# Two Strassen MLPs on one core: block sums of the weights by adding loads, another order of the products, moved embedding parts

## The chip, the cores and the metric

One core of one Trainium2 chip runs the whole kernel. The metric is the device time of one execution in microseconds (us), and fewer is better. Five engines work in parallel, each through its own in-order list of instructions, and wait for each other by semaphores: PE (TensorE, matrix products), DVE (VectorE), ACT (ScalarE), POOL (GpSimd) and SP (SyncE, which only issues transfers here). POOL can issue transfers too.

## The reference

Two transformer blocks follow each other on x of 512 tokens by 1024 features, all in float32. Each has a mixer, which the change leaves alone, and then this:

```python
x = x + merged @ w_out                                   # "wo"
h = rmsnorm(x, g)
x = x + square(relu(h @ w_ff1)) @ w_ff2                  # w_ff1 [1024, 4096], w_ff2 [4096, 1024]
gate = sigmoid(rmsnorm(x, g3) @ w_gate)                  # "pg"
x = x + (p @ w_ple) * gate                               # p [512, 256], the embedding part
```

The second block does the same with weights of its own (`w_mlp1_2`, `w_mlp2_2`, `w_pg_2`, `w_pp_2`), and a final rmsnorm gives the output.

## The kernel before

**Precision.** A float32 product is made of three products of parts with fewer bits: every operand is split into a high part (a copy on ACT: `wh`, `SH`, `XH`, `YH`) and a low part (a subtraction on DVE: `wl`, `SL`, `XL`, `YL`), and PE adds high*high, high*low and low*high in a PSUM bank. Weights arrive as raw chunks of 1 MB (`raw`, two buffers, issued by SP) and are split in units of 128 x 1024 elements. `wh` and `wl` have three buffers (`NW = 3`), so a unit is converted when the unit three ahead of it has been used by PE (`ac_hi`, `dv_lo`, event `wfree`). A unit feeds 24 matmuls, or 12 where it is half of a product.

**First layer.** `dense_mlp` runs the eight blocks of `wo`, then the hidden features in four groups (g = 0 to 3) of eight blocks `f1` each. ACT makes relu and square into `hid`.

**Second layer.** For each group the product of `hid` (512 tokens by 1024) with 1024 rows of `w_ff2` is done by Strassen's method: seven products of quarters (M1 to M7) instead of eight. The weights' quarters lie in four tiles `RB` (11, 12, 21, 22, of 1 MB each), loaded by SP in `sp_second`. Four of the seven products need a sum of two weight quarters; DVE makes it in place (`dv_weight_sums`, two halves each). Four operand sums on DVE (`dv_operands`: into `E` and in place in `hid`) make the other side. `PRODUCTS` gives for each product the pair of banks, whether it starts them afresh (otherwise it adds on), and the quarter of the output `xt` (tokens th, features nh, sign) into which DVE adds the banks (`dv_mlp`, event `f2e`).

The products of group g lie between the `f1` blocks of group g + 1, one after each. The last group has no such blocks: its seven products stand one after another, with two embedding parts (`ple`: one unit, 24 matmuls each) after the third and the sixth.

**Around it.** The rows of p are loaded by POOL (`pl_ple`, tile `prows`), transposed by PE (`pe_ple`) and split into `PPH` and `PPL`. When a quarter of `xt` is complete, PE transposes it (`pe_turn`, order `TURN`), DVE adds it to `XT` (first MLP), and the gate product `pg` follows (`fm_lead`, three blocks which begin with features 4 to 7). In the second MLP the turned quarters are split straight from the banks, and the gate product is `pg2`. The scale `rst1` for the gate comes from squares (ACT), their sum in `ACC` (DVE) and a product with ones; `dv_gate` needs it before it frees a bank.

**Order.** Each engine has lanes of steps (`vector_lanes` and the like). A planner (`arrange`) runs through them with costs and due times of its own and writes out one fixed order for each engine; conversions are due by the place at which PE needs them. A step that waits holds up everything behind it on its engine.

```python
us = [self.unit(self.RB[q][:, 2 * h:2 * h + 2, :], 2, 512, ("rb", blk, g, q) if kind == "rb" else ("ts", blk, g, k, h)) for h in range(2)]
...
if u["i"] >= NW:
    ac.wait_ge(self.at("wfree", u["i"] - NW))
```

## Time and profile before

| | |
|---|---|
| runs before (3) | 1928.93, 1932.8, 1934.3 us, median 1932.8 |
| profiled execution | 1934.82 us |
| its span, first to last instruction | 1933.0 us |
| PE busy | 1883.5 us, 97% |
| PE weight load, beside it | 1551.5 us |
| DVE busy | 1151.1 us, 60% |
| ACT busy | 855.3 us, 44% |
| POOL busy | 98.8 us, 5% |
| mean granted clock | 0.989 |

The profile is of one execution. "Busy" is the time with an instruction of the engine under way. "PEclk" is the granted share of TensorE's full clock in a stage. In a row of a stage the number in brackets behind a busy time is how many instructions started in it. A wait names the engine and the tile that came last. The first MLP lies at about 464 to 866 us, the second at about 1476 to 1878 us.

### The profile page before, as it was taken

To read this page: it belongs to the slowest core of one execution; us is meant where nothing else is said; L and a number is where in the kernel's file an instruction comes from. 1 tells how busy PE (TensorE), PEld (TensorE's weight loads), DVE (VectorE), ACT (ScalarE), POOL (GpSimd) and SP (SyncE) were. 2 spreads that over 40 slices of the span, in tenths; PEclk is the share of its full clock that TensorE was granted. 3 is DMA by queue.
4 is the path that set the end of the run, shared out by engine and by line. 5 is a ranking of instruction groups with operands and counts; after the bars stand their busy time and mean duration, and the time that the engine had idled before them with its cause. 6 is when DMAs were issued, how large, how long until landed. Compare 5 with 4: busy or idle time off the path is not lost.

```text
span 1933.0 us, 23466 instructions
## 1 busy us (share of the span) xinstructions
PE 1883.5 (97%) x9426; PEld 1551.5 (80%) x9426; DVE 1151.1 (60%) x1777; ACT 855.3 (44%) x1318; POOL 98.8 (5%) x153
## 2 busy tenths in 40 slices
PE   7999999998999999899999999999999999999897
PEld 5887778877788888778888888898887888888786
DVE  5769665446456857788734335424345456857775
ACT  6435554323344444456634324333233444445363
POOL 2110111002000000000100000000000000000000
PEclk9999999999999999899999999999999999999999
DMA  6233211129423232212431222232255223232211
GB/s 226 66 91 119 85 55 40 45 78 328 127 66 110 87 131 87 87 44 79 142 117 47 88 69 85 92 105 82 93 196 185 87 66 122 81 124 89 97 44 65
DMA packets 158175, 194.65 MB, mean 101 GB/s; under 512 B 14826, under 2 KB 118932, under 8 KB 158067
## 3 DMA queue, kind: packets, MB, share of 16 engines
q1 hardware_dynamic: 151954, 181.91, 29.2%
q0 software_dynamic: 4528, 8.94, 1.4%
q10 hardware_dynamic: 1584, 2.30, 0.3%
q8 instruction: 75, 1.23, 0.3%
q14 instruction: 34, 0.27, 0.0%
HBM read 179.41 MB, written 15.54 MB: 101 GB/s over the span
## 4 chain that ended last, share of the span: by engine, by line
PE 87%; DVE 7%; ACT 2%; DMA 2%; issue 2%; POOL 0%; POOLq 0%; DVEq 0%; SPq 0%; ACTq 0%
PE bank L131 84%; PE bank L134 3%; DVE wl L155 1%; DMA prows<-in_p_dram 1%; ACT L141 1%; ACT wh L141 1%; DVE ACC L155 1%; DVE T L155 1%; DVE RB L155 0%; DMA scr_x<-XT 0%; DVE XL L163 0%; DVE XT L155 0%; ACT GP L141 0%; DVE ML L155 0%; DVE xt L163 0%
## 5 line engine op out<-in xcount | busy, mean ns | idle before, releaser
L131 PE MATMUL bank<-XH,wh 128*128 128x512 f32 (+1 forms) x1272 | 504.1, 396 | 5.3 <-DVE XL L163 2.2
L131 PE MATMUL bank<-XL,wh 128*128 128x512 f32 (+1 forms) x1272 | 497.0, 391 | 1.0 <-DVE XL L163 1.0
L141 ACT ACTIVATE wh<-raw 128x1024 fp32r<-128x1024 f32 (+1 forms) x239 | 252.8, 1058 | 534.2 <-PE bank L131 526.2
L155 DVE TENSOR_TENSOR wl<-raw,wh 128x1024 fp32r<-128x1024 f32 x238 | 292.8, 1231 | 269.6 <-ACT wh L141 269.1
L131 PE MATMUL bank<-XH,wl 128*128 128x512 f32 x1264 | 318.7, 394 | 0.0
L131 PEld LDWEIGHTS bank<-XH,wh 128*128 128x128 f32 (+1 forms) x1272 | 238.8, 188 | 60.5 <-issue 2.6
L131 PEld LDWEIGHTS bank<-XL,wh 128*128 128x128 f32 (+1 forms) x1272 | 238.9, 188 | 51.0 <-DVE XL L163 2.4
L131 PEld LDWEIGHTS bank<-XH,wl 128*128 128x128 f32 x1264 | 236.3, 189 | 49.6 <-issue 0.6
L141 ACT ACTIVATE wh<-RB 128x1024 fp32r<-128x1024 f32 x112 | 119.1, 1063 | 158.6 <-PE bank L131 158.6
L155 DVE TENSOR_TENSOR wl<-RB,wh 128x1024 fp32r<-128x1024 f32 x112 | 137.0, 1223 | 76.5 <-ACT wh L141 76.4
L131 PE MATMUL bank<-wh,SL 128*128 128x512 f32 x448 | 140.2, 395 | 12.6 <-DVE SL L155 12.6
L131 PE MATMUL bank<-wh,SH 128*128 128x512 f32 x448 | 139.6, 393 | 0.0
L131 PE MATMUL bank<-wl,SH 128*128 128x512 f32 x448 | 139.3, 392 | 0.0
L131 PEld LDWEIGHTS bank<-wh,SL 128*128 128x128 f32 x448 | 85.2, 191 | 31.1 <-DVE SL L155 13.5
L131 PEld LDWEIGHTS bank<-wl,SH 128*128 128x128 f32 x448 | 85.2, 190 | 18.0
L131 PEld LDWEIGHTS bank<-wh,SH 128*128 128x128 f32 x448 | 84.6, 190 | 17.6
L163 DVE SCALAR_TENSOR_TENSOR xt<-bank,scales,xt 128x512 f32<-128x512 f32 x104 | 77.7, 747 | 4.1 <-DVE xt L163 0.9
L155 DVE TENSOR_TENSOR RB<-RB,RB 128x1024 f32<-128x1024 f32 x64 | 78.2, 1221 | 1.4
L155 DVE TENSOR_TENSOR T<-bank,RST 128x512 f32<-128x512 f32 x58 | 40.0, 689 | 60.6 <-PE bank L131 60.3
L131 PE MATMUL bank<-wh,XH 128*128 128x512 f32 x192 | 60.4, 396 | 0.0
L131 PE MATMUL bank<-wh,XL 128*128 128x512 f32 x192 | 59.7, 392 | 0.0
L131 PE MATMUL bank<-wl,XH 128*128 128x512 f32 x192 | 59.7, 392 | 0.0
(446 smaller groups left out, 2583.7 us busy)
## 6 DMA issues: line engine op xcount, KB each, us to landing
raw<-in_w_in_dram SPq DMA_DIRECT2D x58, 1024.0 KB, 5.2
RB<-in_w_ff_dram SPq DMA_DIRECT2D x16, 1024.0 KB, 5.0
raw<-in_w_ff_dram SPq DMA_DIRECT2D x16, 1024.0 KB, 5.3
RB<-in_w_mlp_dram SPq DMA_DIRECT2D x16, 1024.0 KB, 5.1
raw<-in_w_mlp_dram SPq DMA_DIRECT2D x16, 1024.0 KB, 5.3
raw<-in_w_out_dram SPq DMA_DIRECT2D x8, 1024.0 KB, 5.2
scr_x<-XT POOLq DMA_DIRECT2D x16, 256.0 KB, 4.6
XT<-scr_x SPq DMA_DIRECT2D x8, 512.0 KB, 10.9
```

Of the source, the lines that this page charges most:

```text
L131: return self.put(ns, lambda e: e.matmul(out, lhsT, rhs, start=start, stop=stop, skip_group_check=True))
L134: return self.put(109, lambda e: e.transpose(out, in_, ident))
L141: return self.put(ns, lambda e: e.activation(out, in_, func, bias=bias, scale=scale), func)
L155: return self.put(self.ns(out), lambda e: e.tensor_tensor(out, a, b, op))
L163: return self.put(self.ns(out), lambda e: e.scalar_tensor_tensor(out, a, s, b, op0, op1))
```

## The change

- `dv_weight_sums` on DVE goes. In its place POOL issues loads that add to what lies in the tile (`dma_add`, `accum_op`): for each of the four sums the second quarter is read from DRAM again and added to the first in `RB`, in two halves of 512 KB (`pl_weight_sums`, lane `tsum`, in the order sum 1, 3, 2, 4). Sum 3 waits for the load of quarter 12, the others until the low part of the plain weights in the tile has been made.
- The quarters 11 and 12 change tiles from group to group, and SP loads in the order 22, 11, 21, 12.
- The order of the products was M1, M2, M5, M6, M3, M7, M4 and is M1, M5, M6, M3, M7, M2, M4. M2 has banks 4 and 5 and not 6 and 7. The operand sum for M3 is made after the second operand (M6) has been split.
- The embedding parts stand ahead of the first and the second product of the last group. Their raw chunk is planned ahead of that group's products.
- The transposes of `prows` wait for the last block of `wo` too.
- Quarters are turned in the order 12, 22, 11, 21. In the first MLP ACT's squares come in fours behind the copies.
- After the first MLP the ring of banks for `pg` has a fourth one, bank 3.

```diff
--- before.py
+++ after.py
@@ -195,6 +195,13 @@
 
     def idle(self):
         return [self.last] if self.e is not None and self.last else []
+
+    def dma_add(self, out, in_):
+
+        if self.e is None:
+            self.notes.append(("dma", self.dma_ns, 8 * int(np.prod(in_.shape))))
+            return Noted(self.notes)
+        return self.e.dma_start(out, in_, accum_op=ALU.add)
 
     def power(self, out, a, b):
         return self.put(500 + 250 * size(out), lambda e: e.tensor_tensor(out, a, b, ALU.pow))
@@ -533,13 +540,14 @@
         yield from self.fm_lead(s, "Y", [("pg", n) for n in range(3)])
         for n in range(3, 8):
             yield from self.fm(s, "Y", ("pg", n))
+        self.ring = (0, 1, 2)
         yield from self.fm_pair(s, "X2", ("ha",), ("gqk", 0, 0))
         for pr in range(2):
             for c in range(2):
                 for i in range(2):
                     if (pr, c, i) != (0, 0, 0):
                         yield from self.fm(s, "X2", ("gqk", c, 2 * pr + i))
-        yield from self.tm(s, "X2", ("gv", 0), [("xm", 0, 3, 7)])
+        yield from self.tm(s, "X2", ("gv", 0), self.last_use[3])
         yield from self.tm(s, "X2", ("gv", 1), [("free", "gv", 0, 3)])
         for g in range(3):
             for pr in range(2):
@@ -580,11 +588,12 @@
                 yield from self.fm(s, x, ("f1", blk, g + 1, n))
                 if n < 7:
                     yield from self.product(s, blk, g, n)
+
         for i in range(7):
+            if i < 2:
+                yield from self.ple(s, blk, i)
             yield from self.product(s, blk, 3, i)
-            if i in (2, 5):
-                yield from self.ple(s, blk, i == 5)
-        self.ring, self.last_use[2] = (0, 1, 2), self.pair_after[2]
+        self.ring, self.last_use[2], self.last_use[3] = (0, 1, 2) if blk else (0, 1, 2, 3), self.pair_after[2], self.pair_after[3]
 
     def ple(self, s, blk, hf):
         if blk == 0:
@@ -1773,11 +1782,11 @@
     def plan_ff(self, blk, w1, wp):
         for j in range(4):
             self.plan("f1", w1, 0, 8, 256 * j, 256, "n", 2)
-        made = ((11, "rb", 11), (21, "rb", 21), (11, "ts", 1), (11, "ts", 2), (22, "rb", 22), (12, "ts", 3), (21, "ts", 4))
+        made = ((11, "rb", 11), (11, "ts", 1), (11, "ts", 2), (22, "rb", 22), (12, "ts", 3), (21, "rb", 21), (11, "ts", 4))
 
         def product(g, i):
             q, kind, k = made[i]
-            us = [self.unit(self.RB[q][:, 2 * h:2 * h + 2, :], 2, 512, ("rb", blk, g, q) if kind == "rb" else ("ts", blk, g, k, h)) for h in range(2)]
+            us = [self.unit(self.RB[g][q][:, 2 * h:2 * h + 2, :], 2, 512, ("rb", blk, g, q) if kind == "rb" else ("ts", blk, g, k, h)) for h in range(2)]
             self.f2_units.setdefault((blk, g), []).append(us)
         for g in range(3):
             for n in range(8):
@@ -1786,12 +1795,11 @@
                 self.piece(ci, "n", 2, n % 2)
                 if n < 7:
                     product(g, n)
+        ci = self.chunk(wp, 0, 2, 0, 1024)
         for i in range(7):
+            if i < 2:
+                self.piece(ci, "n", 2, i)
             product(3, i)
-            if i == 2:
-                ci = self.chunk(wp, 0, 2, 0, 1024)
-            if i in (2, 5):
-                self.piece(ci, "n", 2, i == 5)
 
     def sp_spill1(self, s):
         sp = self.sp
@@ -1876,7 +1884,10 @@
         self.xt = m("xt", 16, [128, 4, 1024])
         self.SH = [m("SH", 24 + 4 * i, [128, 4, 256], F32R) for i in range(2)]
         self.SL = [m("SL", 26 + 4 * i, [128, 4, 256], F32R) for i in range(2)]
-        self.RB = {q: m("RB", 32 + 4 * i, [128, 4, 512]) for i, q in enumerate((11, 12, 21, 22))}
+
+        RB = [m("RB", 32 + 4 * i, [128, 4, 512]) for i in range(4)]
+        self.RB = [{11: RB[g % 2], 12: RB[1 - g % 2], 21: RB[2], 22: RB[3]} for g in range(4)]
+        self.RB_SLOT = [{11: g % 2, 12: 1 - g % 2, 21: 2, 22: 3} for g in range(4)]
         self.E = self.page("E", P_SCAN, [128, 4, 256])
         YA, YB = [m("YA", 4 * i, [128, 4, 512], F32R) for i in range(2)], [m("YB", 8 + 4 * i, [128, 4, 512], F32R) for i in range(2)]
         self.YH, self.YL = [[YB[i][:, k, :] for k in range(4)] + [YA[i][:, k, :] for k in range(4)] for i in range(2)]
@@ -1907,8 +1918,8 @@
 
 
 
-    PRODUCTS = (("M1", (2, 3), True, 0, 0, 1), ("M2", (6, 7), True, 0, 0, 1), ("M5", (4, 5), True, 1, 1, 1), ("M6", (2, 3), False, 0, 1, -1),
-                ("M3", (4, 5), False, 0, 1, 1), ("M7", (2, 3), False, 1, 1, -1), ("M4", (2, 3), False, 1, 0, 1))
+    PRODUCTS = (("M1", (2, 3), True, 0, 0, 1), ("M5", (4, 5), True, 1, 1, 1), ("M6", (2, 3), False, 0, 1, -1), ("M3", (4, 5), False, 0, 1, 1),
+                ("M7", (2, 3), False, 1, 1, -1), ("M2", (4, 5), True, 0, 0, 1), ("M4", (2, 3), False, 1, 0, 1))
 
     def quarter(self, g, th, kh):
         return self.hid[g % 2][:, 4 * kh:4 * kh + 4, 256 * th:256 * th + 256]
@@ -1916,13 +1927,13 @@
     def operand(self, g, i):
 
         q = self.quarter
-        return (q(g, 0, 0), q(g, 0, 1), self.E[:, :, :], q(g, 0, 0), q(g, 0, 1), q(g, 1, 0), q(g, 1, 1))[i]
+        return (q(g, 0, 0), self.E[:, :, :], q(g, 0, 0), q(g, 0, 0), q(g, 1, 0), q(g, 0, 1), q(g, 1, 1))[i]
 
     def operand_made(self, blk, g, i):
-        tiles = {0: range(4), 1: range(4, 8), 6: range(4, 8)}.get(i)
+        tiles = {0: range(4), 5: range(4, 8), 6: range(4, 8)}.get(i)
         if tiles:
             return [self.at("hid", blk, g, n) for n in tiles]
-        return [self.at("ss", blk, g, {2: 1, 3: 2, 4: 4, 5: 3}[i])]
+        return [self.at("ss", blk, g, {1: 1, 2: 2, 3: 4, 4: 3}[i])]
 
     def ac_operands(self, s):
         ac = self.ac
...
@@ -1955,48 +1966,49 @@
                 dv.wait_ge(s.now())
                 dv.tensor_tensor(q(g, 1, 0), q(g, 0, 0), q(g, 1, 0), ALU.subtract).then_inc(*s.up(("ss", blk, g, 3)))
                 yield
-                self.splitting = x0 + 3
+                self.splitting = x0 + 2
                 dv.wait_ge(s.now(), at("sh", blk, g, 0))
                 dv.tensor_tensor(q(g, 0, 0), E, q(g, 0, 0), ALU.subtract).then_inc(*s.up(("ss", blk, g, 2)))
-                yield
-                low(1)
-                yield
-                self.splitting = x0 + 4
-                dv.wait_ge(s.now(), at("sh", blk, g, 1))
-                dv.tensor_tensor(q(g, 0, 1), q(g, 0, 1), q(g, 0, 0), ALU.add).then_inc(*s.up(("ss", blk, g, 4)))
-                for i in range(2, 7):
+                for i in range(1, 7):
                     yield
                     low(i)
-
-    def dv_weight_sums(self, s):
-
-        dv, at, RB = self.dv, self.at, self.RB
+                    if i == 2:
+                        yield
+                        self.splitting = x0 + 3
+                        dv.wait_ge(s.now(), at("sh", blk, g, 2))
+                        dv.tensor_tensor(q(g, 0, 0), q(g, 0, 1), q(g, 0, 0), ALU.add).then_inc(*s.up(("ss", blk, g, 4)))
+
+    def second(self, blk, g, q, k0=0, nk=4):
+
+        r0, c0 = 1024 * g + 512 * (q // 10 - 1) + 128 * k0, 512 * (q % 10 - 1)
+        return self.a[("w_ff2", "w_mlp2_2")[blk]][0][r0:r0 + 128 * nk, c0:c0 + 512].rearrange("(k p) n -> p k n", p=128)
+
+    def pl_weight_sums(self, s):
+
+        pl, at = self.pl, self.at
         for blk in range(2):
             for g in range(4):
-                part = lambda q, h: RB[q][:, 2 * h:2 * h + 2, :]
                 u = self.f2_units[blk, g]
-                for k, q, a, b, i, lows, loads in ((1, 11, 11, 12, 2, 0, (11, 12)), (3, 12, 12, 22, 5, None, (22,)), (2, 11, 11, 22, 3, 2, ()), (4, 21, 11, 21, 6, 1, (21,))):
+                for k, q, b in ((1, 11, 12), (3, 12, 22), (2, 11, 22), (4, 11, 21)):
                     for h in range(2):
                         yield
-                        self.splitting = u[i][h]
-                        dv.wait_ge(s.now(), *[at("rb", blk, g, x) for x in loads], *([at("lo", u[lows][h])] if lows is not None else []))
-                        dv.tensor_tensor(part(q, h), part(a, h), part(b, h), ALU.add).then_inc(*s.up(("ts", blk, g, k, h)))
+                        pl.wait_ge(at("rb", blk, g, q), *([] if k == 3 else [at("lo", u[{1: 0, 2: 1, 4: 2}[k]][h])]))
+                        pl.dma_add(self.RB[g][q][:, 2 * h:2 * h + 2, :], self.second(blk, g, b, 2 * h, 2)).then_inc(
+                            *self.sig(f"ts{self.RB_SLOT[g][q]}{h}").up16(("ts", blk, g, k, h)))
 
     def sp_second(self, s):
 
         sp, at = self.sp, self.at
-        for blk, name in enumerate(("w_ff2", "w_mlp2_2")):
-            w = self.a[name][0]
+        for blk in range(2):
             for g in range(4):
-                for q in (11, 22, 12, 21):
+                for q in (22, 11, 21, 12):
                     yield
                     if g:
-                        u = self.f2_units[blk, g - 1]
-                        sp.wait_ge(at("lo", u[{11: 3, 22: 4, 12: 5, 21: 6}[q]][1]), *{11: [at("ts", blk, g - 1, 4, 1)], 22: [at("ts", blk, g - 1, 2, 1)], 12: [], 21: []}[q])
+
+                        sp.wait_ge(at("lo", self.f2_units[blk, g - 1][{22: 3, 11: 4, 21: 5, 12: 6}[q]][1]))
                     else:
                         sp.wait_ge(at("l", ("MG", "MG2")[blk], 7), at("acc", ("pa", "ot")[blk], 7))
-                    r0, c0 = 1024 * g + 512 * (q // 10 - 1), 512 * (q % 10 - 1)
-                    sp.dma_start(self.RB[q][:, :, :], w[r0:r0 + 512, c0:c0 + 512].rearrange("(k p) n -> p k n", p=128)).then_inc(*self.sig(f"rb{q}").up16(("rb", blk, g, q)))
+                    sp.dma_start(self.RB[g][q][:, :, :], self.second(blk, g, q)).then_inc(*self.sig(f"rb{self.RB_SLOT[g][q]}").up16(("rb", blk, g, q)))
 
     def dv_mlp(self, s, blk):
         dv = self.dv
...
@@ -2040,23 +2052,23 @@
                 ac.activation(self.hid[g % 2][:, n, :], self.tile["f1", blk, g, n][:, :], ACT.Square).then_inc(*s.up(("hid", blk, g, n)))
 
 
-    TURN = ((11, 1), (12, 4), (22, 5), (21, 6))
+    TURN = ((12, 3), (22, 4), (11, 5), (21, 6))
     TURNED = (4, 5, 6, 7, 0, 1, 2, 3)
 
     def pe_turn(self, s, blk):
         pe = self.pe
-        free = {p: ("f2e", blk, 3, 1, p) for p in range(2)}
+        free = {p: self.FF_FREE[blk] for p in range(2)}
         for q, i in self.TURN:
             th, nh = q // 10 - 1, q % 10 - 1
             for p in range(2):
                 yield
-                pe.wait_ge(*[self.at("f2e", blk, 3, i, j) for j in range(2)], self.at(*free[p]))
+                pe.wait_ge(*[self.at("f2e", blk, 3, i, j) for j in range(2)], *[self.at(*e) for e in free[p]])
                 for f in range(2):
                     for j in range(2):
                         n = 4 * nh + 2 * p + f
                         t = pe.transpose(self.ps[6 + p][:, 256 * f + 128 * j:256 * f + 128 * j + 128], self.xt[:, 2 * th + j, 128 * n:128 * n + 128], self.ident[:, :])
                 t.then_inc(*s.up(("ft", blk, q, p)))
-                free[p] = ("fte", blk, q, p)
+                free[p] = [("fte", blk, q, p)]
 
     def dv_turn(self, s):
         dv = self.dv
...
@@ -2099,6 +2111,12 @@
             yield
             ac.wait_ge(self.at("xm", 0, 3, n))
             ac.copy(self.YH[n], self.XT[:, n, :], self.vec(gain, n)).then_inc(*s.up(("h", "Y", n)))
+            if n in (7, 3):
+                yield from self.ac_squares(s, n - 3)
+
+    def ac_squares(self, s, n0):
+        ac = self.ac
+        for n in range(n0, n0 + 4):
             yield
             ac.wait_ge(self.at("imb", 0), *(self.freed("ysq", n) if n != 4 else []))
             sq = self.tile["ysq", n] if n != 4 else self.ACC
@@ -2110,10 +2128,10 @@
             yield
             dv.wait_ge(self.at("h", "Y", n))
             dv.scalar_tensor_tensor(self.YL[n], self.XT[:, n, :], self.vec(gain, n), self.YH[n].bitcast(F32), ALU.mult, ALU.subtract).then_inc(*s.up(("l", "Y", n)))
-            if n != 4:
-                yield
-                dv.wait_ge(self.at("ysqd", n), s.now())
-                dv.tensor_tensor(self.ACC[:, :], self.ACC[:, :], self.tile["ysq", n][:, :], ALU.add).then_inc(*s.up(("ysa", n)))
+            for m in {7: (5, 6, 7), 3: (0, 1, 2, 3)}.get(n, ()):
+                yield
+                dv.wait_ge(self.at("ysqd", m), s.now(), *([self.at("ysqd", 4)] if m == 5 else []))
+                dv.tensor_tensor(self.ACC[:, :], self.ACC[:, :], self.tile["ysq", m][:, :], ALU.add).then_inc(*s.up(("ysa", m)))
 
 
     def pl_ple(self, s, blk, p):
@@ -2140,7 +2158,7 @@
         pe = self.pe
         for k in range(2):
             yield
-            pe.wait_ge(self.at("prw", blk))
+            pe.wait_ge(self.at("prw", blk), self.at("acc", "wo", blk, 7))
             for j in range(4):
                 t = pe.transpose(self.ps[5 + k][:, 128 * j:128 * j + 128], self.prows[:, j, 128 * k:128 * k + 128], self.ident[:, :])
             t.then_inc(*s.up(("ppT", blk, k)))
...
@@ -3050,7 +3068,6 @@
         yield "onorm", 1000, lambda s: self.chain(self.dv_attn_norm(s), self.dv_gla_norm(s))
         yield "lo", None, self.dv_lo
         yield "operands", None, self.dv_operands
-        yield "sums2", None, self.dv_weight_sums
 
     def scalar_lanes(self):
         yield "norms", 1000, lambda s: self.chain(self.ac_norms(s), self.ac_turn_x(s))
@@ -3079,6 +3096,7 @@
         yield "gna", 0, lambda s: self.pl_group_norm(s, 0)
         yield "gnb", 0, lambda s: self.pl_group_norm(s, 1)
         yield "onorm", 0, lambda s: self.chain(self.pl_attn_norm(s), self.pl_gla_norm(s), self.pl_last(s))
+        yield "tsum", 0, self.pl_weight_sums
         yield "merge", 500, lambda s: self.chain(self.pl_merge(s), self.pl_blank2(s))
         yield "spill", 2000, lambda s: self.chain(self.pl_params(s), self.pl_keep(s), self.pl_ple(s, 0, a["p"][0, 0]), self.pl_rel_bias(s), self.pl_copy_bias(s), self.pl_spill2(s), self.pl_load_bias(s),
                                                   self.pl_dil(s), self.pl_ple(s, 1, a["p_2"][0, 0]), self.pl_lnf(s))
@@ -3166,7 +3184,7 @@
                     return l.slack
                 if l.slack is None:
                     need, lead = {("dv", "lo"): (self.need_lo, 2500), ("ac", "hi"): (self.need, 5000), ("ac", "operands"): (self.s_need, 5000),
-                                  ("dv", "operands"): (self.s_need, 3500), ("dv", "sums2"): (self.need, 9000)}[eng, l.name]
+                                  ("dv", "operands"): (self.s_need, 3500)}[eng, l.name]
                     return max(t, clock["pe"]) + 227 * (need[l.unit_of[l.i]] - dense) - lead
                 return t + l.slack
             lane = min(go, key=due)[1]
```

## Rows read from the trace of the kernel before

**Rows 1.** Page, busy time of each engine over the whole span.

```profile
PE 1883.5 (97%) x9426; PEld 1551.5 (80%) x9426; DVE 1151.1 (60%) x1777; ACT 855.3 (44%) x1318; POOL 98.8 (5%) x153
```

**Rows 2.** Waits of PE: for whom, total us, times, longest us.

```profile
PE bank L131 <- DVE SL L155: 12.6, 2, 6.3
PE bank L134 <- DMA prows<-in_p_dram: 8.2, 2, 5.3
...
PE bank L134 <- DVE xt L163: 1.9, 2, 1.7
```

**Rows 3.** Stages at two last groups: time, engines' busy us (starts), PEclk, DMA share, GB/s.

```profile
812.00:816.00 4.00, 0.00 (x0) 0.00 (x0) 3.98 (x4) 0.00 (x0) 0.00 (x0) 0.50 0.00 0
816.00:820.00 4.00, 3.97 (x9) 3.15 (x10) 2.36 (x2) 0.00 (x0) 0.00 (x0) 0.50 0.02 4
820.00:824.00 4.00, 4.00 (x15) 3.21 (x14) 2.21 (x3) 1.06 (x1) 0.00 (x0) 0.74 0.00 0
...
1828.00:1832.00 4.00, 2.98 (x7) 2.40 (x8) 3.32 (x3) 0.00 (x0) 0.35 (x1) 0.50 0.00 0
1832.00:1836.00 4.00, 4.00 (x18) 3.25 (x18) 1.73 (x2) 1.15 (x2) 0.20 (x1) 0.95 0.39 133
```

**Rows 4.** Timeline, DVE and PE around the first SL wait: start, us.

```profile
811.83 0.74 DVE L163 SCALAR_TENSOR_TENSOR xt<-bank,scales,xt 128x512 f32<-128x512 f32 x1
812.49 1.22 DVE L155 TENSOR_TENSOR RB<-RB,RB 128x1024 f32<-128x1024 f32 x1
813.62 1.22 DVE L155 TENSOR_TENSOR hid<-E,hid 128x1024 f32<-128x1024 f32 x1
814.76 1.22 DVE L155 TENSOR_TENSOR SL<-hid,SH 128x1024 fp32r<-128x1024 f32 x1
...
816.03 1.22 PE L131 MATMUL bank<-wh,SL 128*128 128x512 f32 x2 [6.32 <-DVE SL L155]
...
826.68 1.03 PE L134 MATMUL bank<-ident,xt 128*128 128x128 f32 x8
```

**Rows 5.** Stages around the transposes of prows, both MLPs (columns as above).

```profile
470.00:475.00 5.00, 2.87 (x11) 2.68 (x12) 0.93 (x2) 1.20 (x2) 0.00 (x0) 0.55 1.05 362
475.00:480.00 5.00, 5.00 (x15) 2.66 (x14) 2.98 (x5) 3.14 (x4) 0.00 (x0) 0.77 0.83 304
...
1480.00:1485.00 5.00, 2.08 (x10) 1.51 (x9) 0.00 (x0) 0.00 (x0) 0.00 (x0) 0.92 1.05 385
1485.00:1490.00 5.00, 5.00 (x21) 4.28 (x20) 2.57 (x4) 2.79 (x5) 0.00 (x0) 0.73 1.05 387
```

**Rows 6.** Page, groups of instructions on the RB tiles.

```profile
L141 ACT ACTIVATE wh<-RB 128x1024 fp32r<-128x1024 f32 x112 | 119.1, 1063 | 158.6 <-PE bank L131 158.6
L155 DVE TENSOR_TENSOR wl<-RB,wh 128x1024 fp32r<-128x1024 f32 x112 | 137.0, 1223 | 76.5 <-ACT wh L141 76.4
...
L155 DVE TENSOR_TENSOR RB<-RB,RB 128x1024 f32<-128x1024 f32 x64 | 78.2, 1221 | 1.4
```

**Rows 7.** Stages: one undisturbed group, and the first MLP's last group.

```profile
640.00:721.60 81.60, 81.60 (x361) 67.57 (x360) 57.94 (x55) 39.14 (x45) 0.00 (x0) 1.00 0.32 103
...
805.80:866.00 60.20, 53.13 (x232) 42.78 (x230) 50.49 (x54) 30.98 (x38) 0.00 (x0) 0.91 0.06 18
```

**Rows 8.** DMA issues: count, KB each, median us to landing.

```profile
RB<-in_w_ff_dram SPq DMA_DIRECT2D x16, 1024.0 KB, 5.0
...
raw<-in_w_proj_b_dram SPq DMA_DIRECT2D x4, 512.0 KB, 3.7
...
scr_b<-scr_row POOLq DMA_DIRECT2D x2, 512.0 KB, 14.2
...
scr_b<-scr_row POOLq DMA_DIRECT2D x1, 768.0 KB, 5.7
```

**Rows 9.** Instructions on scr_b: duration ns, first and last start, time to landing.

```profile
L119 POOL DMA_DIRECT2D scr_b<-scr_row x3: 1082/1109/1162, 484.4 to 486.7; - x3
...
DMA to landing us min/median/max: 4.6/5.8/16.7
```

More of the change, by code:

```diff
@@ L1949, in dv_operands @@
                 yield
-                self.splitting = x0 + 2
+                self.splitting = x0 + 1
                 dv.wait_ge(s.now(), at("sl", blk, g, 0), at("ppT", blk, 1), *[at("hid", blk, g, n) for n in range(8)])
@@ L2193, in pe_norms @@
         yield from self.pe_turn(s, 0)
-        yield from self.pe_mean_squares(s, "rst1", self.ACC, self.ps[4], ("ysa", 3), ("ysqd", 4), ("f2e", 0, 3, 4, 0))
+        yield from self.pe_mean_squares(s, "rst1", self.ACC, self.ps[4], ("ysa", 3), ("ysqd", 4), ("f2e", 0, 3, 5, 0))
         yield from self.pe_spread(s, "rst1", self.T[2], self.ps[4], ("ms1",))
         yield from self.pe_mean_squares(s, "m1", self.ACC, self.ps[4], ("sqp", 7), ("rst1",))
-        yield from self.pe_mean_squares(s, "m2", self.ACC2, self.ps[5], ("sqp2", 7), ("f2e", 0, 3, 4, 1))
+        yield from self.pe_mean_squares(s, "m2", self.ACC2, self.ps[5], ("sqp2", 7), ("f2e", 0, 3, 5, 1))
         yield from self.pe_spread(s, "rstB", self.T[2], self.ps[4], ("m1",))
```

14 lines of the change are left out of this document (7 added, 7 removed).

## The prediction

> **What bounds the kernel now.** I read the busy shares first. TensorE (PE) is busy 97% of the span [rows 1], so time can only come out of PE's own idle time or its slow clock, and a saving on another engine counts only where PE waits for it. So the next view is who PE waited for [rows 2]: 12.6 us in two waits for SL (the low half of an operand, from VectorE), 8.2 us in two waits for the load of prows (the embedding rows), 1.9 us in two waits for xt (VectorE's eviction of the last product). These are 22.7 of PE's 49.5 idle us (1933.0 less 1883.5), and all three lie in the code that is changed.
>
> A wait costs more than its idle time, because the granted clock falls. The stages around the first SL wait show it: no matmul from 812 to 816, clock 0.50 until past 820, 0.74 to 824 [rows 3]. In an undisturbed group PE starts 361 matmuls in 81.6 us [rows 7], 0.226 us each, so a block of 24 takes 5.4 us. From 816.0 to 824 there are 24 where 5.4 us would do: 2.5 us lost at half clock, the 1.2 GHz level. In the second MLP 25 start between 1829.0 and 1836: 1.3 us lost [rows 3]. In the same way 18 matmuls and 8 transposes (8 in about 0.9 us at full clock [rows 4]) fill 472.1 to 480, where 5.0 us would do: 2.9 us lost; in the second MLP 31 starts take 7.1 us where 6.1 would do: 1.0 us lost [rows 5]. The waits and their slow clock together: 12.6 + 3.8 + 8.2 + 3.9 = 28.5 us.
>
> **Why PE waits for SL.** The timeline in front of the wait shows VectorE in one unbroken queue: an eviction (811.8), a weight sum RB (812.5), an operand sum (813.6), and only then SL of the second product (814.8), for which PE sits idle 6.3 us [rows 4]. The same rows give the price of a piece in such a queue, start to start: 0.66 us for an eviction, 1.14 for a piece of 1024 elements. The last group has no f1 blocks between its products, so VectorE is needed at twice the rate.
>
> **The sums leave VectorE.** 64 sums of 1.22 us go, 78 us of VectorE [rows 6]. In groups 0 to 2 that is worth nothing: there VectorE is busy 58 of 81.6 us and PE 81.6 of 81.6 [rows 7]. In the last group two things remove the SL wait: the weight sum in the queue goes, and, more important, the first embedding block now lies ahead of product 0 and the second between products 0 and 1. hid is complete some 4 us before product 0 starts (f1 block 7 ends 5.4 us ahead, relu and square take 1.3), SL of product 1 then follows E, two sums and at most five other pieces, about 10 us, that is at +6 us, and product 1 starts at +10.9. Worth both waits and their clock: 12.6 + 3.8 = 16.4 us.
>
> What the denser end costs: from the start of product 1 PE has 6 products (32.6 us) and three turned quarters (16 transposes, 1.9 us each), 38 us. VectorE has in it 13 splits wl, 5 SL and one operand sum (1.14 each), 10 evictions and 4 YL (0.66 each), 6 additions to XT and 3 to ACC (0.6 each, an estimate from the eviction's size): 21.7 + 9.2 + 5.4 = 36.3 us. That is 95%; before, it was 50.5 of 60.2 us with the idle time of the wait in it [rows 7]. Bounds 0 and 4 us per MLP; I take 1.
>
> **The sums become adding loads.** Eight per group, 512 KB each, issued by GpSimd, whose queue is empty in both MLPs. The trace has no adding load. Its cost has two parts: a fixed latency, and an occupancy X by which the next one is later. A plain MB lands in 5.0 us, a plain half MB in 3.7 [rows 8]; I take 1.45 us per half MB and 2.1 fixed. If the add means that the target is read as well, two passes make 2.9 and three 4.4. The slowest row on this queue are the three copies scr_b, 1.75 MB from DRAM to DRAM, issued from 484.4 to 486.7 and landed within 16.7 us of issue: 19 us, less 2.1, is 4.8 us per half MB, with other loads beside them [rows 8, 9]. So X lies between 1.45 and 4.8; I take 3: source and target kind are those of the plain load, with one more pass. The issue itself is some 0.8 us of an idle engine.
>
> What waits for them: weight halves are converted three units ahead (wh has 3 buffers, and ScalarE's conversions of RB waited 158.6 us, all for PE [rows 6]). With product 0 at S: its two low halves are made at S-5.8 and S-3.0 (a unit is freed, then 1.06 + 1.22 + 0.1 us; S-8.5 for the first in the last group). The GpSimd lane is in order: sum 1 (two halves), sum 3 (two), sum 2. Sum 2's first half is needed 1.3 us before product 2: at S+20.5 in groups 0 to 2, at S+15.0 in the last. The backlog lands it at S-3.7+5X and S-0.9+4X: in time up to X = 4.8 and X = 4.0. At X = 3 it arrives 4 us early in the last group. Cost 0. Extra traffic: 4 MB per group of 81.6 us beside a DMA share of 0.32 [rows 7]; weight chunks are fetched about 24 us ahead of their use and land in 5, so nothing of PE's moves.
>
> "Collectives: The Full Stack" of the Trainium skill (The bandwidth ceiling) says that an add in the DMA path is slow not for the add but for its two source reads, about half the rate of a copy. By it X would be about 2.9 us, an estimate from that page; no trace here shows it.
>
> **The transposes of prows wait for the last wo product.** Before, they stood in PE's order where the load was still under way. Now PE goes on with wo, seven more blocks, some 38 us; the load, 5.3 us late before, has landed long by then. Gain 8.2 + 3.9 = 12.1 us. What is late next: wo's weights are fetched as far ahead as all chunks; the bias copies (scr_b) move with the transposes, to the start of f1, where a chunk beside them may take as long as they did, 16.7 us [rows 9], inside its 24. PPH and PPL have eight f1 blocks, 44 us, before a product asks for the banks. Cost 0.
>
> **Product order, turn, fourth bank.** Same matmuls and evictions. M7 and M4, on the same banks, are no longer neighbours. The quarters for chunks 4 to 7 are now finished at product 4 instead of 5, so the first gate half has its inputs 5.4 us earlier and can cover the last eviction, where PE waited 1.9 us: gain 0 to 3 with its share of the issue gaps, I take 1.5. ScalarE's squares are put after the copies, which makes rst1 2 to 3 us later; bank 3 lets PE do one more gate block (5.4 us) meanwhile. Cost 0, and without that bank some 2 us.
>
> **Sum.** 16.4 + 12.1 + 1.5 - 2 = 28 us. The profiled execution took 1934.8 (span 1933.0): 1906.8. It is 2.0 above the median of the runs, so the forecast is 1905. Its own range is 1899 to 1912.
>
> **Rivals.** (a) *The last group's wait comes back as a wait for sum 2.* X between 4.0 and 5: at 4.8 the half lands at S+18.3, 3.3 us late, with a slow clock 6.3 us, twice: 1905 + 13 = 1918. For it: the lane's fixed order and the densest place. Against it: X would have to be near that of DRAM-to-DRAM copies. Chance 0.16. (b) *VectorE still sets the end.* At 95% its splits come late: 4 us per MLP and clock, 1905 + 10 = 1915. Chance 0.11. (c) *Slower: adding loads are a stream too slow for the products.* One mechanism, in every group: X above 4.8 makes groups 0 to 2 wait as well. At 5.2: last groups 2 x (4.9 + 3), others 6 x 2.3: 30 us, which eats the gain; from there on it is slower. At 6: 2 x 11 + 6 x 8.8 = 75, so 1980. The bound of the rows is only 8% below the turning point; the doubled plain load is far below it. Chance 0.13. (d) *The prows change only moves a wait*, into the join of wo and f1, where PE has gaps already: 12 us less, 1917. Chance 0.06.
>
> **How the numbers follow.** Likeliest 0.54. The range, 1896 to 1923, takes in (a), (b), (d) and the likeliest: 0.87 less its tails. Runs of this kernel differ by about 0.3% (5.8 us), so 1927 and 1939 part the signs. Faster: 0.54 + 0.14 + 0.11 + 0.05 = 0.84; same 0.05; slower 0.11.
>
> **What would show it.** In the profile after: no RB<-RB,RB on VectorE, which is 78 us less busy; 64 adding issues on GpSimd's queue with a time to landing near 5 to 6 us (above 8: (a) or (c)); no PE wait for SL at the start of the last groups; no PE wait for prows; PE's busy time lower by the clock's 7.7 us; the clock at 1.00 in these stages. ScalarE's conversions of RB would still wait for PE; if they wait for a DMA, the adds are late. What would make me wrong: a long add, VectorE's order in the last six products, or the written-out order of another lane shifting a wait to where I don't look.

## The result, and the profile after

| | before | after |
|---|---|---|
| median | 1933.36 us (4 runs, 1928.93 to 1934.3) | 1907.17 us (4 runs, 1906.6 to 1908.02) |
| profiled execution, span | 1934.82, 1933.0 us | 1908.02, 1906.2 us |
| mean granted clock | 0.989 | 0.995 |

The ratio is 0.9869, with a 95% interval of 0.9852 to 0.9886: 26 us less, where 28 were forecast. The predicted time was 1905 us.

The busy line of the page, against [rows 1]:

```profile
PE 1876.2 (98%) x9426; PEld 1546.0 (81%) x9426; DVE 1081.1 (57%) x1713; ACT 853.9 (45%) x1318; POOL 177.0 (9%) x217
```

PE's idle time is 1906.2 - 1876.2 = 30.0 us and was 49.5, that is 19.5 less. Its busy time is 7.3 us less for the same 9426 matmuls; the forecast had 7.7 for the clock. The sum is the 26.8 us between the spans. VectorE is 70 us less busy, where 78 were forecast: the 64 sums went, at 1.1 us each from start to start and not the 1.22 of their own duration.

The waits of PE (for whom, total us, times, longest us), against [rows 2]:

```profile
PE bank L134 <- DMA ident<-in_c_ident_dram: 5.0, 1, 5.0
PE bank L131 <- DVE XL L163: 4.7, 3, 2.2
...
PE bank L131 <- ACT XH L141: 1.4, 1, 1.4
...
PE bank L131 <- DVE wl L155: 1.1, 1, 1.1
...
PE bank L134 <- DVE xt L163: 0.4, 1, 0.4
```

Two lines of the same list in the kernel before, which [rows 2] leaves out:

```profile
PE bank L131 <- DVE XL L163: 3.1, 3, 2.2
...
PE bank L131 <- DVE XT L155: 1.6, 2, 0.8
```

SL and prows are gone from the list, and xt fell from 1.9 to 0.4 us. The waits for XT are gone too: they stood at the join of wo and f1, 0.8 us in each MLP. The wait for the identity matrix is at the start and was there before. New, and small, are XH (1.4 us) and one wait for a low half wl (1.1 us) in the second MLP's last group. XL rose from 3.1 to 4.7 us. XH and the rise of XL lie behind the gate product of the first MLP, where the second block begins (start, us, engine, what, idle before):

```profile
902.22 0.43 PE L131 MATMUL bank<-XH,wh 128*48 128x512 f32 x1 [1.38 <-ACT XH L141]
904.59 0.44 PE L131 MATMUL bank<-XL,wh 128*48 128x512 f32 x1 [1.94 <-DVE XL L163]
```

The stages, with the columns of [rows 3]: the place of the old prows wait in both MLPs [rows 5], one undisturbed group [rows 7], and the last six products of each MLP.

```profile
470.00:475.00 5.00, 5.00 (x24) 4.14 (x23) 4.28 (x6) 2.48 (x4) 0.00 (x0) 1.00 1.05 358
475.00:480.00 5.00, 5.00 (x24) 4.14 (x23) 2.83 (x5) 1.60 (x3) 0.00 (x0) 1.00 1.06 375
632.00:713.60 81.60, 81.60 (x361) 67.59 (x361) 49.35 (x47) 39.11 (x46) 9.74 (x8) 1.00 0.63 154
...
811.30:850.20 38.90, 38.75 (x183) 31.66 (x182) 33.72 (x39) 22.02 (x25) 2.41 (x2) 1.00 0.37 68
1480.00:1485.00 5.00, 5.00 (x24) 4.14 (x23) 3.13 (x4) 2.20 (x3) 0.00 (x0) 1.00 0.31 107
1485.00:1490.00 5.00, 5.00 (x24) 4.14 (x23) 3.27 (x4) 2.20 (x3) 0.00 (x0) 1.00 0.18 51
1813.00:1852.00 39.00, 37.55 (x178) 30.55 (x177) 31.73 (x40) 26.69 (x45) 2.37 (x2) 1.00 0.38 77
```

Where 11 and 15 starts stood there are 24 and 24, at full clock. In the last six products PE is idle 0.15 us in the first MLP and 1.45 in the second, and the clock is 1.00, where it had fallen to 0.50. In the undisturbed group PE is as busy as before, VectorE has 49.4 us in place of 57.9 and GpSimd 9.7, and the DMA share has doubled from 0.32 to 0.63.

What the second product of the last group waited for now stands early in VectorE's queue. Its SL and its first matmul in the first MLP:

```profile
800.89 1.22 DVE L155 TENSOR_TENSOR SL<-E,SH 128x1024 fp32r<-128x1024 f32 x1
...
811.43 0.62 PE L131 MATMUL bank<-wh,SH 128*128 128x512 f32 x2
```

The page on the new loads: the queue on which GpSimd issues (packets, MB, share of the 16 engines), and the issues with their median time to landing, beside the plain loads of RB [rows 8]:

```profile
q0 software_dynamic: 21936, 42.49, 12.0%
...
RB<-in_w_ff_dram SPq DMA_DIRECT2D x16, 1024.0 KB, 5.1
...
RB<-in_w_ff_dram POOLq DMA_DIRECT2D x32, 512.0 KB, 7.7
...
RB<-in_w_mlp_dram POOLq DMA_DIRECT2D x32, 512.0 KB, 8.0
```

### The profile page after: what moved, and what is told of

It is laid out like the page before. It is cut to its first block, busy times and chain, and to the rows that moved or that the text cites. A ratio compares the mean times of both kernels' runs of the same rounds, so it can differ in the third digit from the quotient of the medians.

```text
span 1906.2 us, 23419 instructions
## 1 busy us (share of the span) xinstructions
PE 1876.2 (98%) x9426; PEld 1546.0 (81%) x9426; DVE 1081.1 (57%) x1713; ACT 853.9 (45%) x1318; POOL 177.0 (9%) x217
## 3 DMA queue, kind: packets, MB, share of 16 engines
q0 software_dynamic: 21936, 42.49, 12.0%
## 4 chain that ended last, share of the span: by engine, by line
PE 90%; DVE 4%; ACT 2%; DMA 2%; issue 1%; SPq 0%; POOLq 0%; ACTq 0%; DVEq 0%
PE bank L131 88%; PE bank L134 2%; DVE wl L155 1%; DMA raw<-in_w_in_dram 1%; ACT L141 1%; ACT wh L141 1%; DVE XL L163 1%; DVE T L155 0%; DMA RB<-in_w_ff_dram 0%; DMA xs<-in_x_dram 0%; DVE ACC L155 0%; ACT GP L141 0%; DVE xt L163 0%; DVE XT L155 0%; ACT T L141 0%
## 5 line engine op out<-in xcount | busy, mean ns | idle before, releaser
L131 PEld LDWEIGHTS bank<-wl,SH 128*128 128x128 f32 x448 | 83.9, 188 | 19.5 <-DVE wl L155 2.1
L204 POOL DMA_DIRECT2D RB<-in_w_mlp_dram x32 | 38.4, 1383 | 321.5 <-DVE wl L155 321.5
L204 POOL DMA_DIRECT2D RB<-in_w_ff_dram x32 | 38.9, 1404 | 270.0 <-DVE wl L155 270.0
```

The source lines that it names most:

```text
L131: return self.put(ns, lambda e: e.matmul(out, lhsT, rhs, start=start, stop=stop, skip_group_check=True))
L204: return self.e.dma_start(out, in_, accum_op=ALU.add)
```

## The experiments

The experiments ran in three sets, each with the kernel before beside it: its medians are 1931.3, 1931.1 and 1931.8 us. "Less than before" is counted from the one of the same set.

### The two moved waits, one at a time

```diff
 # e1: the kernel before, and
-            pe.wait_ge(self.at("prw", blk))
+            pe.wait_ge(self.at("prw", blk), self.at("acc", "wo", blk, 7))
```

> The kernel before, with one edit: the transposes of prows wait for the last wo product too. Theory (the wait is removed, with its slow clock): PE's wait for prows of 8.2 us goes and PE's clock is full in both stages, so 12.1 us less than before, about 1921 us. Rival (the wait only moves into the join of wo and f1): within 4 us of before, with new PE waits for XL, XH or PPH at the join. The SL waits of 12.6 us stay in both.

Measured: 1918.93 us (1917.53 to 1922.51), ratio 0.994 (0.9925 to 0.9955), 12.4 us less than before. The waits of PE:

```profile
PE bank L131 <- DVE SL L155: 12.7, 2, 6.3
...
PE bank L131 <- DVE XL L163: 3.1, 3, 2.2
...
PE bank L134 <- DVE xt L163: 1.7, 1, 1.7
```

prows is out of the list, nothing came in for it, XL and xt are the 3.1 and 1.7 us that they were or near it, and SL is untouched. The predicted term was 12.1 us. The wait was removed and not moved. At the join, where the rival looked for a new wait, one went: XT, 1.6 us before, is out of the list too. PE's busy time fell by 3.0 us (1883.5 to 1880.5), which is the clock's part.

```diff
 # e5: the kernel before, and
         for i in range(7):
+            if i < 2:
+                yield from self.ple(s, blk, i)
             yield from self.product(s, blk, 3, i)
-            if i in (2, 5):
-                yield from self.ple(s, blk, i == 5)
...
+        ci = self.chunk(wp, 0, 2, 0, 1024)
         for i in range(7):
+            if i < 2:
+                self.piece(ci, "n", 2, i)
             product(3, i)
-            if i == 2:
-                ci = self.chunk(wp, 0, 2, 0, 1024)
-            if i in (2, 5):
-                self.piece(ci, "n", 2, i == 5)
```

> The kernel before, with one edit: the two embedding parts of the last group stand ahead of its first and second product. The sums stay on VectorE, the order of the products stays. Theory P (place: the wait for SL goes because product 1 starts 5.4 us later behind the finished hid): the two SL waits shrink from 6.3 us each to under 1.5, 12 to 16 us less than before, about 1918 us, though the end of the group is denser and may take 2 to 6 us back. Theory A (adds: it goes because VectorE is rid of the sums): the waits shrink by at most half, 1925 us or more.

Measured: 1920.47 us (1919.91 to 1923.77), ratio 0.9949 (0.9934 to 0.9964), 10.9 us less, a little under the 12 to 16 of theory P. The waits of PE:

```profile
PE bank L134 <- DMA prows<-in_p_dram: 7.8, 2, 4.8
...
PE bank L131 <- DVE YA L163: 2.0, 1, 2.0
PE bank L134 <- DVE xt L163: 1.7, 2, 1.3
```

Both SL waits are gone with the sums still on VectorE. So it is the place of the embedding parts that removes them. What comes back is a wait of 2.0 us for YA (the low parts of the gate's operand) at the end of the first MLP; xt was waited for there before as well (1.7 us, now 1.3). The new wait brings its own slow clock, in a stage that was at 1.00 before (columns as above):

```profile
860.00:864.00 4.00, 3.95 (x8) 2.62 (x9) 3.79 (x6) 3.36 (x6) 0.00 (x0) 0.50 0.00 0
```

```diff
 # e9: the kernel before with both edits of e1 and e5
```

> The kernel before with two edits only: the transposes of prows wait for the last wo product, and the embedding parts stand ahead of the first and second product of the last group. Theory (two waits, two edits; adding loads, product order and fourth bank give nothing or little): the gains of the two alone (12.4 and 10.9 us) add up, 1908 us, and what is left to the changed kernel, 0 to 3 us, belongs to the order of the products and the turn (the last eviction and the splits of Y that waited 2.0 us in the kernel with the parts moved alone). Rival (the rest of the change carries more): 1911 us or more.

Measured: 1907.67 us (1904.80 to 1909.98), ratio 0.9876 (0.9862 to 0.9889), 24.2 us less. The changed kernel, run beside it (below), has 0.9872. The waits of PE:

```profile
PE bank L131 <- DVE YA L163: 2.4, 2, 2.0
PE bank L134 <- DVE xt L163: 1.7, 2, 1.3
```

The two gains add up, 12.4 + 10.9 = 23.3, and the two edits alone reach the changed kernel within what can be measured. YA and xt, 2.4 and 1.7 us here, are what the order of the products and the turn take away in the changed kernel (0 and 0.4). The sums are not what does it: the next kernel has them on VectorE, and 0.2 us for each. In the time of the kernel this isn't resolved, 1907.7 against 1906.6 us with ranges that overlap.

### What the adding loads are worth

```diff
 # e2: the changed kernel, and (lane "sums2" of DVE again, lane "tsum" of POOL gone)
+                for k, q, b, i, lows, loads in ((1, 11, 12, 1, 0, (11, 12)), (2, 11, 22, 2, 1, (22,)), (3, 12, 22, 4, None, ()), (4, 11, 21, 6, 2, (21,))):
+                    for h in range(2):
...
+                        dv.tensor_tensor(part(q, h), part(q, h), part(b, h), ALU.add).then_inc(*s.up(("ts", blk, g, k, h)))
...
 # sp_second waits for these sums too before it loads 22 and 21 again
```

> The changed kernel, with the adding loads taken back: the eight half sums per group are made by VectorE in the order 1, 2, 3, 4, everything else as changed. Theory P: PE waits less than 5 us more than in the changed kernel, 1907 to 1913 us. Theory A: VectorE has 9.8 us more work in the last group, which was at 95% by the count of the prediction (36.3 of 38 us), so PE waits there 6 to 10 us in each MLP and 1922 us or more. My count says that 95% plus 5.7 us (five of the eight half sums fall behind the start of product 1) is 110%: I lean to something between, 1915.

Measured: 1905.92 us (1905.84 to 1907.09), ratio 0.9871 (0.9857 to 0.9886). The adding loads give nothing. The last six products of both MLPs, columns as above:

```profile
811.00:850.00 39.00, 38.87 (x183) 32.02 (x182) 38.90 (x45) 22.09 (x25) 0.00 (x0) 1.00 0.04 14
1813.00:1852.00 39.00, 38.59 (x185) 31.54 (x184) 38.03 (x46) 28.21 (x48) 0.00 (x0) 1.00 0.06 18
```

In the first MLP VectorE is busy 38.9 of 39.0 us and PE still 38.87. The queue is full from end to end, and PE waits for nothing of it: the sums fill the 5.2 us in which VectorE was idle in the changed kernel, and every split and SL is still made before PE asks for it. I had leaned to 1915 us for this kernel, from a count of 110%; that was wrong.

```diff
 # e3: the changed kernel, with the embedding parts behind the third and sixth product again (e5 reversed)
```

> The changed kernel, with the embedding parts put back behind the third and sixth product of the last group; the adding loads stay. Theory P: PE waits again before product 1 (SL or a weight half), and sum 1, which now has 5.4 us less, waits for its load: 7 to 15 us more than the changed kernel, 1914 to 1922 us. Theory A: under 3 us more, 1907 to 1910.

Measured: 1914.62 us (1908.86 to 1916.02), ratio 0.9907 (0.9887 to 0.9927). That lies at the lower edge of theory P's range. Lines of the timeline of the first MLP (start, us, engine, what, idle before):

```profile
801.20 1.03 PE L131 MATMUL bank<-wh,SL 128*128 128x512 f32 x2 [2.02 <-DVE SL L155]
...
808.18 1.06 ACT L141 ACTIVATE SH<-hid 128x1024 fp32r<-128x1024 f32 x1 [7.08 <-PE bank L131]
809.14 1.99 ACT L141 ACTIVATE wh<-RB 128x1024 fp32r<-128x1024 f32 x2
...
810.28 0.69 PE L131 MATMUL bank<-wh,SH 128*128 128x512 f32 x2 [2.20 <-issue]
```

PE waits 2.0 us for SL, and 2.2 us at 810.3 for which the profile names no one. The lines show whom: the conversion of wh (809.1) stands in ScalarE's order behind an SH (808.2) that had waited for PE, and PE starts when its first half has ended. The order is the planner's, written out by its own costs, and on the chip it is late here.

```diff
 # e12: e2 and e3 together
```

> The changed kernel with both taken back: the sums on VectorE and the embedding parts behind the third and sixth product. With the two kernels that take back one each, and the changed kernel, this fills a table of four. Theory (the adding loads are worth something only where the parts are not moved): SL is waited for again, 4 to 7 us per MLP with the slow clock, 1918 to 1924 us, against 1914.6 with adding loads. Rival (adding loads give nothing anywhere): within 2 us of 1914.6.

Measured: 1919.9 us (1917.84 to 1922.93), ratio 0.9942 (0.9929 to 0.9954), 5.3 us above e3. PE's wait for SL:

```profile
PE bank L131 <- DVE SL L155: 14.1, 2, 7.0
```

The four cells, as ratios to the kernel before:

| | sums by adding loads | sums on VectorE |
|---|---|---|
| embedding parts at products 0 and 1 | 0.9869 (0.9852 to 0.9886) | 0.9871 (0.9857 to 0.9886) |
| embedding parts behind products 2 and 5 | 0.9907 (0.9887 to 0.9927) | 0.9942 (0.9929 to 0.9954) |

The adding loads take some 5 to 7 us off only where the SL wait exists, and there not all of it. Where the parts are moved there is no wait left for them to remove.

### What an adding load costs

```diff
 # e7: the changed kernel, and
-        return self.e.dma_start(out, in_, accum_op=ALU.add)
+        return self.e.dma_start(out, in_)
```

> The changed kernel, but the loads overwrite the first quarter and do not add (the weight sums are left out of the computation, so the products use the second quarter alone). The same bytes from DRAM by the same queue. Theory (the add costs a second pass): the median landing falls from 7.7 us to about 4 to 5, and the DMA engines' share in the MLPs falls, while the time of the kernel stays within 3 us, since nothing of PE's hangs on the landing. Rival (the slow landing comes from the issuing queue and not from the add): landing stays above 7 us.

This kernel leaves the sums out of what it computes. Measured: 1906.64 us (1906.35 to 1908.59), ratio 0.9875 (0.986 to 0.9889). The queue in the kernel before, and then the queue and the median landing in this one, from the pages:

```profile
q0 software_dynamic: 4528, 8.94, 1.4%
...
q0 software_dynamic: 13744, 42.49, 6.7%
...
RB<-in_w_mlp_dram POOLq DMA_DIRECT2D x32, 512.0 KB, 4.1
```

The instructions that touch RB, of which the issues (times, duration of one in ns: least, median, longest):

```profile
L204 POOL DMA_DIRECT2D RB<-in_w_ff_dram x32: 708/712/755, 545.3 to 818.6; - x32
```

The occupancy X can be read from the shares. GpSimd's queue had 1.4% of the engines' span before. With the adds it has 12.0%: (12.0 - 1.4)% of 1906.2 us is 202 us for 64 loads, 3.16 us each. Plain: (6.7 - 1.4)% of 1904.5 us is 101 us, 1.58 us each. The add costs twice the plain load, as a second pass would, and it moves the same 42.49 MB in more packets: (21936 - 4528) / 64 = 272 for each load in place of 144. The issue takes 1.2 us in place of 0.71, and the median landing 8.0 in place of 4.1 us. None of this reaches PE, whose one wait for wl stays at 1.1 us. The lines around it, in the last group of the second MLP of this kernel:

```profile
1812.03 1.05 ACT L141 ACTIVATE wh<-RB 128x1024 fp32r<-128x1024 f32 x1
...
1815.62 0.75 DVE L163 SCALAR_TENSOR_TENSOR xt<-bank,scales,xt 128x512 f32<-128x512 f32 x1 [5.01 <-PE bank L131]
...
1817.64 1.22 DVE L155 TENSOR_TENSOR wl<-RB,wh 128x1024 fp32r<-128x1024 f32 x1
...
1818.91 0.74 PE L131 MATMUL bank<-wl,SH 128*128 128x512 f32 x2 [1.07 <-DVE wl L155]
```

The high half wh is ready at 1813.1, and VectorE is idle for 5.0 us. But its order has two evictions ahead of the split wl, and these wait for PE. In the changed kernel the same wh comes 3.3 us later against these evictions, since ScalarE waits 3.2 us for its load, and PE's wait is the same 1.1 us. So it is the place of one split in VectorE's order that PE waits for, and not the adding load.

```diff
 # e6: the changed kernel, and in front of each adding load
+                        if last:
+                            pl.wait_ge(at(*last))
+                        last = ("ts", blk, g, k, h)
```

> The changed kernel, but each adding load is issued only when the one before it has landed, so that each occupies the lane for its whole time to landing and its issue, about 6.4 + 1.2 = 7.6 us. By the prediction's formula (in time up to an occupancy of about 5, slower than before from 5.2) sum 2 is some 12 us late in groups 0 to 2 and 17 us late in the last: 2000 us or more, with ScalarE's conversions waiting for the loads. Rival (the lane's backlog is not what counts, since the first sums start early enough): under 15 us more than the changed kernel.

Measured: 1992.21 us (1990.29 to 1993.55), ratio 1.0315 (1.0299 to 1.033), 61 us more than before and 85 more than the changed kernel. That is a little less than the 2000 us or more that was expected, since the adds follow each other faster than the 7.6 us assumed. GpSimd's timeline in the second group (start, us, engine, what):

```profile
636.61 1.20 POOL L204 DMA_DIRECT2D RB<-in_w_ff_dram  x1 [42.68 <-DVE wl L155]
643.40 1.21 POOL L204 DMA_DIRECT2D RB<-in_w_ff_dram  x1 [5.58 <-DMA RB<-in_w_ff_dram]
650.20 1.20 POOL L204 DMA_DIRECT2D RB<-in_w_ff_dram  x1 [5.59 <-DMA RB<-in_w_ff_dram]
```

The waits of PE in the whole of this kernel ("issue" is time for which the profile names no one):

```profile
PE bank L131 <- issue: 43.4, 8, 10.3
PE bank L131 <- ACT wh L141: 13.7, 8, 2.6
```

One add follows the other after 6.8 us, since each waits for the landing of the one ahead. PE waits 57.1 us in 16 places, twice in each of the 8 groups, behind wh; the rest of the loss, 28 us, goes with a mean granted clock of 0.980 in place of 0.995. This is rival (c) on the chip. The prediction's lines for the second sum, at X = 6.8 and without the fixed 2.1 us, which is inside this X, give it 7.7 us late in groups 0 to 2 and 9.2 in the last; with 3 us of slow clock each that is 6 x 10.7 + 2 x 12.2 = 89 us, and 85 were measured. This fit was made after the run, with the measured 6.8, and its parts agree less well than its sum: the waits by the formula are 64.6 us and 57.1 were measured, in groups 0 to 2 3.5 to 7.4 us each and in the last ones 12.1 and 10.9. So the mechanism is shown, a backlog of adds that is longest in the last group, and the formula is good for the size only. That the turning point lies at 5.2 was not tried.

### Order of the adds, and the fourth bank

```diff
 # e8: the changed kernel, and
-                for k, q, b in ((1, 11, 12), (3, 12, 22), (2, 11, 22), (4, 11, 21)):
+                for k, q, b in ((1, 11, 12), (2, 11, 22), (3, 12, 22), (4, 11, 21)):
```

> The changed kernel, with the adding loads issued in the order of their use, sum 1, 2, 3, 4 in place of 1, 3, 2, 4. Sum 2 then has no backlog of sum 3 in front of it: ScalarE's waits for loads (13.1 us in the changed kernel) shrink to under 3 us, and the small PE waits in the last groups behind them (about 1 us) go: 0 to 2 us less than the changed kernel. Rival (these waits of ScalarE cover nothing of PE's): within 0.5 us.

Measured: 1905.25 us (1904.91 to 1905.53), ratio 0.9865 (0.985 to 0.988). It was run again beside the changed kernel:

> The changed kernel as it is, on the same chip and in the same rounds as the others of this call, so that differences of 1 to 2 us can be read: 1907 us.

> The changed kernel with the adding loads in the order 1, 2, 3, 4, against the changed kernel in the same rounds: 1.5 to 2.5 us less, 1905 us, if the earlier difference (1905.25 against 1907.17 us, in different calls) is real; within 0.5 us if it lay in the calls.

Measured: the changed kernel 1906.57 us (1905.42 to 1908.53), 0.9872 (0.9858 to 0.9885); with the other order 1905.01 us (1903.22 to 1905.95), 0.9864 (0.9849 to 0.9879). Twice the lower median, by 1.9 and 1.6 us, but the intervals overlap, so the gain stays open; it is the fastest version seen. PE's wait of 1.1 us for wl is gone from both of its traces: with this order of the loads the planner puts that split ahead of the two evictions. ScalarE's waits for these loads in the changed kernel (for whom, total us, times, longest us):

```profile
ACT wh L141 <- DMA RB<-in_w_mlp_dram: 6.7, 5, 3.2
...
ACT wh L141 <- DMA RB<-in_w_ff_dram: 6.4, 4, 2.4
```

The same waits with the other order, 3.4 us in all where under 3 was expected:

```profile
ACT wh L141 <- DMA RB<-in_w_ff_dram: 1.8, 1, 1.8
...
ACT wh L141 <- DMA RB<-in_w_mlp_dram: 1.6, 1, 1.6
```

```diff
 # e4: the changed kernel, and
-        self.ring, ... = (0, 1, 2) if blk else (0, 1, 2, 3), ...
+        self.ring, ... = (0, 1, 2), ...
```

> The changed kernel, with three banks in place of four for the gate product after the first MLP. Theory (rst1 comes later now, the fourth bank covers it): PE waits 1 to 3 us for a bank (a T from VectorE) before the fourth gate block, 1908 to 1910 us. Rival (rst1 is early enough): within 0.5 us of the changed kernel.

Measured: 1907.67 us (1906.39 to 1911.62), ratio 0.9875 (0.9859 to 0.9892). PE's timeline behind the first MLP:

```profile
867.12 0.95 PE L131 MATMUL bank<-ones,ACC 128*128 128x1 f32 x8
871.05 0.66 PE L134 MATMUL bank<-ident,T 128*128 128x128 f32 x4 [2.99 <-DVE T L166]
873.19 3.78 PE L131 MATMUL bank<-YB,wh 128*128 128x512 f32 x8 [1.48 <-DVE T L155]
```

Between the product with ones (867.1) and the next gate block PE waits 3.0 us for T, the spread of the scale, and 1.5 us for the eviction that needs it. The mechanism is there in the profile, 4.5 us of it, and the median moved by only 0.5 us (1.1 against the second runs of the changed kernel), less than the theory asked for. A reason stands further on in the same trace, where the second block begins:

```profile
911.44 0.43 PE L131 MATMUL bank<-XL,wh 128*48 128x512 f32 x1 [0.35 <-DVE XL L163]
```

Here PE waits 0.35 us for XL and not at all for XH; the changed kernel has 1.9 and 1.4 us at this place. So the fourth bank takes 4.5 us of waits away and brings 3.0 back some 30 us later, 1.5 us in all. The profiled execution was the slowest of the four (1911.62; the others 1906.4 to 1907.7), and 1.6 us of that are a longer wait for LD far ahead of the change, which is between 0 and 3.0 us in the traces of these kernels. A gain of the fourth bank isn't shown in the times.

## Why the prediction was right

**The bound and the size.** The reading of PE's waits with their slow clock as what there is to win was right: 28.5 us of waits and clock counted, 26 to 27 gained. That the number came out doesn't speak for the reasoning on the adding loads: the kernel with the two moved waits alone (e9) is at 1907.7 us, and a forecast without a word on the loads would have come as close.

**The prows term.** 12.1 us predicted, 12.4 measured by e1 alone. The closeness is in part luck: the waits that went are 9.8 us and not 8.2, since XT at the join went too, and the clock gave 3.0 us and not 3.9. Rival (d) is out.

**The SL term.** 16.4 us predicted. The profile after has none of the wait. SL of the second product is ready at 802.1 us, 1.8 us behind the start of product 0 (800.35) where 6 was predicted, and product 1 starts at +11.1 where +10.9 was. The 1.8 comes with the new order of the products, whose second one takes the operand sum that is made first; with the old order (e5) this SL is ready at +6.4. As an edit by itself (e5) the place gives 10.9 us, with a new wait of 2.0 us and its slow clock at the end of the first MLP; put into the changed kernel with the sums on VectorE (e12 to e2) it gives 0.9942 - 0.9871, some 14 us. The prediction named two causes for it and called the place of the parts the more important. The runs go further: it is the only one that is needed. "The weight sum in the queue goes" is worth nothing beside it; without it, it is worth the 5 to 7 us of e12 against e3.

**The denser end.** Predicted: VectorE at 95%, 1 us lost per MLP, bounds 0 and 4. Measured: 33.7 of 38.9 us, 87%, with 0.15 and 1.45 us lost. The term was right in size, but the count behind it is 2.6 us too high, and the step from it to a loss was wrong: e2 has VectorE at 99.7% of this stretch in the first MLP and PE waits no more, and in the second MLP 1.1 of the 1.45 us come from the place of one split and not from the load on VectorE. Rival (b) took a busy share for a bound.

**The adding loads.** X was put at 3 us between 1.45 and 4.8; it is 3.16, and the plain load's 1.45 is 1.58. The fixed part is larger than the 2.1 us taken: a lone add lands in 5.9 to 6.4 us, which leaves 2.7 to 3.2, 1.2 of it the issue, where 0.8 was taken. The median landing, 7.7 and 8.0 us, is above the 5 to 6 that the prediction named as its sign, and just short of the 8 that was to speak for (a) or (c). "In time up to X = 4.0, 4 us early" in the last group failed: there ScalarE did wait for sum 2's load, 2.4 us in the first MLP and 3.2 in the second (ScalarE's waits, above). By the prediction's signs "the adds are late" then; they were late for ScalarE and not for PE, since with plain loads (e7) ScalarE waits for none of them and the kernel takes the same time. The price was 0 in the sum, and nothing above 0.3 us of idle PE in the last groups is seen of it.

What the Trainium skill says in "Collectives: The Full Stack" (The bandwidth ceiling) of the reduce step of collectives, half the rate of a copy because of two source reads, agrees with the ratio measured here for a local load: 3.16 to 1.58 us. That it is the reads that cost was not tried.

**Order, turn, fourth bank.** 1.5 us predicted; the waits for xt and YA at the end of the MLP show such a gain (e9 against the changed kernel: 4.1 us of waits against 0.4), and part of it goes again in the 3.0 us for XL and XH; the times don't resolve it. The fourth bank, "some 2 us" by the prediction, is 1.5 us net in the trace.

**What was left out.** XL and XH at the start of the second block took 3.0 us more, for which the prediction had 0. With three banks (e4) the 3.0 us are gone, with the sums on VectorE (e2) they stay, and e1 and e9 don't have them: it is the fourth bank that brings them, since PE now comes to this place before XH and XL are made. Against them stand the 1.6 us for XT, which weren't counted either.

## What to carry to other kernels

Before work is moved to another engine, ask whether it is its place in the order that is late: here two embedding parts, put where the queue was late, gave all that the new loads were meant to give, and the loads added nothing. An engine that is busy to the last tenth is a bound only if something that PE needs stands too late in its queue, and an engine that is idle can still be late, if its order makes it wait for something else first (the split behind two evictions). In a chain of transfers in a fixed order look at what stands ahead of the first that is needed: here adds that landed in 8 us cost nothing while they overlapped, and 85 us when each had to wait for the one ahead. A wait that is taken away early can come back at the next join (the fourth bank), so compare the whole list of waits and not only the one that was aimed at.

## What the runs showed of the hardware

- An adding load of 512 KB from DRAM into SBUF holds the 16 DMA engines 3.16 us, a plain one on the same queue 1.58. It takes 272 packets in place of 144. Its issue keeps GpSimd 1.2 us, against 0.71. A lone one lands 5.9 to 6.4 us after its issue, against 3.9 to 4.2.
- Eight such loads doubled the DMA share of a group (0.32 to 0.63) and left PE's and ScalarE's rows of it as they were.
- After the wait of 6.3 us PE's granted clock was 0.50 (1.2 GHz) from 812 to past 820 us, around the one of 5.3 us it was 0.55 in the stage of 5 us. Waits of 2.0 and 2.2 us were followed by half clock too: 0.68 and 0.61 in the stages of 4 us in e3 (800 to 804 and 812 to 816), and 0.50 from 860 to 864 in e5. Around the wait of 1.1 us in the changed kernel it stayed at 1.00 (1813 to 1852).
